# A two-block transformer stack on one core: gates as row tiles, values in turn, column sums in streamed form, and beta in VectorE's product ahead of the triangular solve

## What is computed

```python
# first block, recurrence: gates from two block-diagonal products of 64 x 64 blocks
r = sigmoid(block_diag(w_rg_r) @ x + b_rg_r)
i = sigmoid(block_diag(w_rg_i) @ x + b_rg_i)
# second block, mixer 0: gated delta rule, 8 heads of 128, chunks of 128 tokens
beta = sigmoid(b_raw)
g = -exp(a_log) * softplus(a_raw + dt_bias)          # b_raw, a_raw: 16 columns of hn @ w_in
gc = cumsum(g)
decay = exp(where(tri_incl, gc[:, None] - gc[None, :], -inf))
a_low = where(tri_strict, (k * beta) @ k.T * decay, 0)
sol = triangular_solve(a_low + eye, [v * beta, k * beta * exp(gc)], unit_diagonal=True)
```

## Time and profile before

| | |
|---|---|
| median of 3 runs | 1115.27 us (1115.21 to 1115.76) |
| profiled execution, its own time | 1115.75 us |
| its span, first to last instruction | 1114.0 us |
| TensorE busy, granted clock | 1103.2 us (99%), 0.998 of full speed |
| VectorE, ScalarE, GpSimd busy | 778.9, 596.5, 218.5 us |
| HBM read | 185.29 MB |

### The profile page before, as it was taken

One profiled execution on the slowest core, in us unless ns is written; L12 is line 12 of the kernel. 1 busy time (PEld: TensorE's weight loads), 2 busy tenths in 40 slices (PEclk: granted clock), 3 DMA queues, 4 the chain that ended last, 5 costly groups with the idle time before them and its releaser, 6 DMA issues.

```text
span 1114.0 us, 19328 instructions
## 1 busy us (share of the span) xinstructions
PE 1103.2 (99%) x7596; PEld 1012.0 (91%) x7596; DVE 778.9 (70%) x969; ACT 596.5 (54%) x806; POOL 218.5 (20%) x222
## 2 busy tenths in 40 slices
PE   9999999999999999999999999999999999999997
PEld 8999998889888889999999888888899999888887
DVE  7746985886877754599985877764467667777444
ACT  6547557645555543665764556643354446665332
POOL 2995003302000000167854010000010002000001
PEclk9999999999999999999999999999999999999999
DMA  9764442755555555445500356555545444656541
GB/s 287 240 219 152 154 140 89 229 185 188 190 188 188 188 193 189 148 138 188 176 29 1 114 172 197 191 195 188 189 152 189 152 151 151 204 190 210 189 151 39
DMA packets 155057, 187.28 MB, mean 168 GB/s; under 512 B 6608, under 2 KB 143984, under 8 KB 154992
## 3 DMA queue, kind: packets, MB, share of 16 engines
q1 hardware_dynamic: 151152, 183.80, 50.8%
q10 hardware_dynamic: 3840, 2.57, 0.8%
HBM read 185.29 MB, written 1.07 MB: 167 GB/s over the span
## 4 chain that ended last, share of the span: by engine, by line
PE 91%; DVE 4%; ACT 2%; POOL 2%; issue 1%; DMA 0%; POOLq 0%; SPq 0%; DVEq 0%; ACTq 0%
PE PS L475 24%; PE PS L525 12%; PE PS L480 12%; PE PS L406 7%; PE PS L407 7%; PE PS L408 7%; PE PS L527 6%; PE PS L354 2%; DVE WL L402 2%; PE PS L486 1%; PE PS L487 1%; PE PS L485 1%; PE PS L2165 1%; PE PS L2152 1%; PE PS L818 1%; DVE QKV L1725 1%
## 5 line engine op out<-in xcount | busy, mean ns | idle before, releaser
L402 DVE TENSOR_TENSOR WL<-RAW,WH 128x2048 fp32r<-128x2048 f32 x169 | 393.9, 2332 | 188.0 <-ACT WH L393 187.3
L393 ACT ACTIVATE WH<-RAW 128x2048 fp32r<-128x2048 f32 x169 | 323.1, 1912 | 190.8 <-PE PS L527 121.1
L475 PE MATMUL PS<-XHL,WH 128*128 128x512 f32 x976 | 336.4, 395 | 0.2 <-DVE WL L402 0.2
L480 PE MATMUL PS<-XHL,WL 128*128 128x256 f32 x976 | 261.6, 277 | 0.0
L475 PEld LDWEIGHTS PS<-XHL,WH 128*128 128x128 f32 x976 | 179.1, 188 | 38.1 <-DVE WL L402 0.4
L525 PE MATMUL PS<-HHL,WH 128*128 (+1 forms) x592 | 205.4, 394 | 0.0
L406 PE MATMUL PS<-XHL,WH 128*128 128x256 f32 x656 | 189.1, 288 | 0.0
L480 PEld LDWEIGHTS PS<-XHL,WL 128*128 128x128 f32 x976 | 183.3, 188 | 5.0
L407 PE MATMUL PS<-XHL,WH 128*128 128x256 f32 x656 | 185.5, 283 | 0.0
L408 PE MATMUL PS<-XHL,WL 128*128 128x256 f32 x656 | 185.5, 283 | 0.0
L527 PE MATMUL PS<-HHL,WL 128*128 (+1 forms) x592 | 164.0, 277 | 0.0
(11 more groups left out here) (345 smaller groups left out, 1695.1 us busy)
## 6 DMA issues: line engine op xcount, KB each, us to landing
RAW<-in_mlp_w_up SPq DMA_DIRECT2D x32, 1024.0 KB, 5.4
RAW<-in_mlp_w_down SPq DMA_DIRECT2D x32, 1024.0 KB, 4.9
RAW<-in_w_in SPq DMA_DIRECT2D x24, 1024.0 KB, 5.3
RAW<-in_w_ffn_in_pairs SPq DMA_DIRECT2D x22, 1024.0 KB, 5.1
RAW<-in_dn_w_in SPq DMA_DIRECT2D x16, 1024.0 KB, 5.8
RAW<-in_mb_w_in SPq DMA_DIRECT2D x12, 1024.0 KB, 5.2
RAW<-in_w_ffn_out SPq DMA_DIRECT2D x11, 1024.0 KB, 4.9
RAW<-in_w_in SPq DMA_DIRECT2D x16, 256.0 KB, 6.3
```

What stands on the lines that cost most here:

```text
L393: act.activation(WH[:, k], RAW[:, k], ACT.Copy).then_inc(hi_done, 1)
L402: dve.tensor_tensor(WL[:, k], RAW[:, k], WH[:, k].bitcast(F32), ALU.subtract).then_inc(lo_done, 1)
L475: pe.matmul(out, h[:, k, part], both[:, k].rearrange("p e t -> p (e t)"), start=(k == 0), stop=False, skip_group_check=True)
L480: mm = pe.matmul(out[:, TOK:512], l[:, low, part], both[:, low, 0], start=False, stop=(low == KB - 1), skip_group_check=True)
```

## The change

1. `WRI` holds, for each half of a block's rows, the two 64 x 64 blocks side by side, with their order swapped in the lower half. Two matmuls of 64 rows replace the two of 128; each writes a bank of its own (`gate_bank`). ScalarE reads four sigmoids of 64 x 256 a step. GpSimd no longer zeroes `WRI`, and SP doesn't wait for that.
2. In the value products of pairs 0 to 7 the heads alternate term by term.
3. The third norm's sums and beta's and decay's columns become one group of 16 matmuls, 32 output columns each (`WBS`) in four column tiles, over the squares and `H`, behind chunk 0. ScalarE copies the bank to `CS`; four small matmuls with a selection matrix (`SEL`) add the four tiles and turn them, in chunk 1 ahead of its tenth matmul. The rows (L662) come behind chunk 1 instead of in its middle. GpSimd prepares `SEL` and `WBS`.
4. The cumulative sum goes behind chunk 3, its copy behind VectorE's read-out of that step, its exponential to step 4 and `BEG` to step 5. TensorE's and VectorE's loops over dq are written out.
5. GpSimd's four products with `BRK2` go; VectorE multiplies key products, `BRK2` and `AM` in one instruction per system, 16 in all.
6. VectorE's read-out of the last dz bank goes behind two of the four odd-column steps, the small product ahead of them. TensorE waits for each bank where it uses it. ScalarE writes the even columns behind the third pair of exponentials, and three of the four silus stand inside the solve.

```diff
-    WRI = sb("WRI", [P, 2, KB, P], F32, Z + 72.25)
+    WRI = sb("WRI", [P, KB, P], F32, Z + 72.25)
+    WBS = sb("WBS", [P, KB, 32], F32, Z + 95)
+    CS = sb("CS", [P, 2, TOK], F32, Z + 84)
...
-        ROWS_AT = [4, 3, 2, 3, 4, 3]
+        ROWS_AT = [4, 3, 3, 3, 4, 3]
...
             elif m == 2:
+                pe.wait_ge(s_.prep, 1)
                 pe.wait_ge(s_.sq_done, 4 * m + 4)
-                for c in range(TT):
-                    for j in range(KB):
-                        mm = pe.matmul(PS[:, 4, 2 * c:2 * c + P].rearrange("p (r e) -> p r e", e=2), XN[:, j, c * P:(c + 1) * P],
-                                       W2[:, j, None, :].to_broadcast([P, P // 2, 2]), start=(j == 0), stop=(j == KB - 1))
+                for r, x in enumerate((XN, H)):
+                    for i in range(2):
+                        for g in range(4):
+                            mm = pe.matmul(PS[32 * g:32 * g + 32, 4, r * TOK:(r + 1) * TOK], WBS[:, 4 * i + g], x[:, 4 * i + g],
+                                           start=(i == 0), stop=(i == 1))
+                mm.then_inc(s_.col_sums, 1)
+                return
...
+        def column_sums(pe):
+            pe.wait_ge(s_.col_out, 1)
+            for c in range(TT):
+                mm = pe.matmul(PS[:, 4, 2 * c:2 * c + 2], CS[:, 0, c * P:(c + 1) * P], SEL[:, 16:18], start=True, stop=True)
+            mm.then_inc(s_.sum_done, 1)
+            for c in range(TT):
+                mm = pe.matmul(PS[:, 3, 256 + 16 * c:272 + 16 * c], CS[:, 1, c * P:(c + 1) * P], SEL[:, 0:16], start=True, stop=True)
+            mm.then_inc(s_.ba_done, 1)
...
         def norm_root(act, m):
+            if m == 2:
+                act.wait_ge(s_.col_sums, 1)
+                act.activation(CS[:].rearrange("p r t -> p (r t)"), PS[:, 4, :], ACT.Copy).then_inc(s_.col_out, 1)
...
+            order = [(e, b) for b in range(3) for e in range(2)] if n < 8 else [(e, b) for e in range(2) for b in range(3)]
+            for e, b in order:
+                mm = term(e, b, slice(P, TOK) if b else slice(0, P), b < 2, b != 1)
...
-            pool.wait_ge(s_.brk, 1)
-            for g in range(4):
-                am = AM[:, 4 * g:4 * g + 4]
-                pool.wait_ge(s_.d_done, 2 * g + 1)
-                pool.tensor_tensor(am, am, BRK2[:, 4 * g:4 * g + 4, None].to_broadcast([P, 4, P]), ALU.mult).then_inc(s_.ab_done, 1)
...
-                sigmoid(RR[:, j], PS[:, 3 + j % 2, 0:TOK], vec("b_rg_r", j)).then_inc(s_.gates_done, 1)
-                sigmoid(RI[:, j], PS[:, 3 + j % 2, TOK:512], vec("b_rg_i", j)).then_inc(s_.gates_done, 1)
+                for r, (out, bias) in enumerate(((RR, "b_rg_r"), (RI, "b_rg_i"))):
+                    for e in range(2):
+                        at = 64 * (r ^ e)
+                        rows_ = slice(64 * e, 64 * e + 64)
+                        sigmoid(out[rows_, j], PS[at:at + 64, gate_bank(j, e), 0:TOK], vec(bias, j)[rows_]).then_inc(s_.gates_done, 1)
...
                 if st.i is None and st.j == 1:
                     act.wait_ge(s_.ba_done, 1)
+                    act.wait_ge(s_.rc_ready, 3)
...
+                        if g == 0:
+                            even_columns()
...
+            gate_silu(0)
...
+                if 2 <= n < 5:
+                    gate_silu(n - 1)
...
                 dve.wait_ge(s_.gk_done, g + 1)
-                dve.wait_ge(s_.ab_done, g + 1)
-                dve.tensor_tensor(AM[:, r], AM[:, r], four(UB[g]), ALU.mult).then_inc(s_.a_done, 1)
-            steps(dve, seg["dq"], dq, head=3, tail=3)
+                dve.wait_ge(s_.d_done, 2 * g + 1)
+                for e in range(4):
+                    n = 4 * g + e
+                    ins = dve.scalar_tensor_tensor(out=AM[:, n], in0=four(UB[g])[:, e], scalar=BRK2[:, n:n + 1], in1=AM[:, n],
+                                                   op0=ALU.mult, op1=ALU.mult)
+                ins.then_inc(s_.a_done, 1)
+            steps(dve, seg["dq"], dq, head=6, tail=3)
...
+            dve.wait_ge(s_.l2sd, 1)
+            ch(dve.tensor_tensor(BRK[:], BETA[:], RK[:], ALU.mult))
             ch.wait(dve)
             dve.wait_ge(s_.ty_even, 1)
             for g in range(4):
+                if g == 2:
+                    gate_rows(Step(seg["dz"], 3, None))
                 dve.wait_ge(s_.ct_done, g + 1)
...
-                    pe.wait_ge(s_.gates_done, 2 * j - 2)
-                for r in range(2):
-                    mm = pe.matmul(PS[:, 3 + j % 2, r * TOK:(r + 1) * TOK], WRI[:, r, j], XN[:, j], start=True, stop=True)
+                    pe.wait_ge(s_.gates_done, 4 * j - 4)
+                for e in range(2):
+                    rows_ = slice(64 * e, 64 * e + 64)
+                    mm = pe.matmul(PS[:, gate_bank(j, e), 0:TOK], WRI[rows_, j], XN[rows_, j], start=True, stop=True)
```

More of the change, by code:

```diff
@@ L834, in attn_pv, with term @@
                 pe.wait_ge(s_.ol_done, 9 if n == 11 else n)
[L835 to L840, removed]
+            pt = turned_to(n)
+            two_heads = list(heads(n))
+            def term(e, b, out, start, stop):
+                _, _, _, vc, to = two_heads[e]
+                return pe.matmul(to[:, out], VT[:, b // 2, vc], queries(pt[:, e, P * b:P * b + P], n), start=start, stop=stop,
+                                 skip_group_check=True)
+            order = [(e, b) for b in range(3) for e in range(2)] if n < 8 else [(e, b) for e in range(2) for b in range(3)]
+            for e, b in order:
+                mm = term(e, b, slice(P, TOK) if b else slice(0, P), b < 2, b != 1)
             mm.then_inc(s_.pv_done, 1)
@@ L1341, in dq @@
                     act.activation(AROW[:], AROW[:], ACT.Exp).then_inc(s_.sm_ready, 1)
-                if st.i is None and st.j == 2:
+                if st.i is None and st.j == 4:
                     act.wait_ge(s_.gc_done, 1)
@@ L1378, in _, with gate_silu @@
                             act.activation(d[:, 4 * g:4 * g + 4], d[:, 4 * g:4 * g + 4], ACT.Exp).then_inc(s_.d_done, 1)
[L1380 to L1382 removed]
+                        if g == 0:
+                            even_columns()
             act.wait_ge(s_.brk, 1)
             act.activation(RK[:], RK2[:], ACT.Sqrt).then_inc(s_.l2sd, 1)
[L1386 removed]
+            def gate_silu(j):
                 zs = ZS[:, 2 * j:2 * j + 2]
@@ L1815, in _ @@
                         key_products(g)
[L1816 to L1817 removed]
+                    break
+                gate_rows(st)
                 if st.j < 2:
@@ L2005, in body @@
                     multiply(pe, st, XH, XL, None if st.j else (s_.xl_ready, 4 * m), tokens_out,
-                             between=lambda: norm_point(pe, m, 2 * st.j))
+                             between=lambda: norm_point(pe, m, 2 * st.j),
+                             beside=(lambda: column_sums(pe)) if m == 2 and st.j == 1 else None)
                     norm_point(pe, m, 2 * st.j + 1)
@@ L2085, in dq @@
                 times_x(2)(st)
-                if st.i is None and st.j == 1:
-                    for c in range(TT):
-                        for k in range(KB):
-                            mm = pe.matmul(PS[:, 3, 256 + 16 * c:384 + 16 * c].rearrange("p (r e) -> p r e", e=16),
-                                           H[:, k, c * P:(c + 1) * P], WBA[:, k, None, :].to_broadcast([P, KB, 16]),
-                                           start=(k == 0), stop=(k == KB - 1))
-                    mm.then_inc(s_.ba_done, 1)
-                if st.i is None and st.j == 2:
+                if st.j == 3:
                     pe.wait_ge(s_.g_ready, 1)
                     pe.matmul(PS[:, 3, 320:336], TRI[:], GT[:], start=True, stop=True).then_inc(s_.gc_sum, 1)
-            steps(pe, seg["dq"], dq, head=3, tail=3)
+            steps(pe, seg["dq"], dq, head=6, tail=3)
             for st in (Step(seg["dz"], j, None) for j in range(4)):
@@ L2129, in _, with banks_free @@
                 mm.then_inc(s_.ct_done, 1)
-            for k in range(SLOTS):
+            def banks_free(k):
                 pe.wait_ge(freed[k], uses_upto(seg["dz"], k))
             def level_x(n):
+                if n == 0:
+                    banks_free(2)
                 pe.wait_ge(s_.yf_out, n + 1)
```

78 lines of the change are left out of this document (41 added, 37 removed).

## The result

The changed kernel takes 1109.31 us (median of 5 runs, 1109.25 to 1109.55), the kernel before on the same chip 1115.41 us: a ratio of 0.9945 (95% interval 0.9935 to 0.9956), 6.1 us less. Its profiled execution took 1109.55 us with a span of 1107.8 us, 6.2 us under the span of before, at a granted clock of 0.999.

A forecast was written before the change was run, and what follows sets the result against it. TensorE, at 91% of the span, was taken to bound the kernel. Savings of 1.1 (gates), 2.1 (values), 1.45 (sums) and 1.75 us (z to the solve) sum to 6.4 us: 1115.27 to 1108.9 us, range 1105.6 to 1112.6.

The forecast's parts named there:

- Gates in row tiles: qk loop: two half-array matmuls take 0.72 us instead of 0.86, eight steps save 1.1 us (0.2 to 3.4).
- Values in turn: Value products of eight head pairs: alternating heads removes a 0.28 us offset, saving 2.1 us (0.8 to 3.4).
- Streamed sums: Third mixer's sums, beta and decay columns: TensorE gives back 3.9 us, of which 1.45 us comes through (0.3 to 3.9).
- Rival 2: Third mixer: TensorE gets the whole of the sums, 3.9 us instead of 1.45, giving 1106.4 us; chance 0.12.
- z to the solve: Last z chunk to second packed product: idle time behind GpSimd's beta products goes, saving 1.75 us (0.7 to 1.9).
- Rival 4: Before the solve: VectorE's 16 products take 1.45 us each, making the kernel slower at 1126.4 us; chance 0.03.
- Rival 1: Third mixer's chunks: VectorE keeps all the time freed by the sums, total gain 4.95 us, 1110.3 us; chance 0.16.
- Rival 3: Gates and values: mode switch leaves row tiles 0.2 us, values stay as they are; 1111.1 us, chance 0.16.

The follow-up runs named there:

- The pairs: Changed kernel with the gate matmuls of two steps together behind every second chunk, one array switch for both: 1110.87 us, ratio 0.9958 to the kernel before.
- squares first: Changed kernel with ScalarE's square of the keys ahead of the tap that waits for VectorE's last read-out: 1108.95 us, ratio 0.9940 to the kernel before.

## Why the prediction was right

The time came out 0.4 us above the forecast of 1108.9 us, well inside the range. The mechanisms are in the main the ones that it named, but part of the closeness is luck: the gates gave 0.8 us less than forecast, and 0.15 us more from the sums, 0.2 us more from the stretch into the solve and 0.27 us at the start, which the change does not explain, made up for most of it. By its steps:

**Gates in row tiles: right in sign, a quarter of the size.** 0.3 us instead of 1.1. The failed step is the choice of 0.72 us from the interval 0.72 to 0.84. The trace has 0.63 us from the gates to the next chunk, 0.09 us more ahead of them and 0.1 us behind: 0.82 us against 0.86. The argument for the low end, that the tiled sums of 256 columns carry an overhead of 0.3 us, was taken from a switch to column tiles; the scores, the only row-tiled block of before, pointed to the other end, and the overhead did not shrink with the columns. The pairs measure it apart: a second pair of gates behind the same switch adds 0.43 us, so the block is 0.43 us of columns and 0.4 us of switch. Here the rule of the Trainium skill quoted with the prediction (TensorEngine Tiling (Array Packing), Key Properties) agrees with the trace, and the sum by it, 0.2 us, was nearer to the measured 0.3 us than mine.

**Values in turn: right.** 0.27 us a step (1.08 to 0.81), eight times, and putting back the order alone gives it back.

**Streamed sums: the total right, its parts not.** 1.6 us for 1.45. The tiled block took 455.81 - 453.94 + 0.09 and 0.1, 2.06 us for 2.05. The small matmuls took 0.9 us instead of 1.2 (457.80 - 456.99, and 0.08): priced from one that stood alone. Each is two records in the profile, and in a row these start every 0.09 us at 2 columns and every 0.11 us at 16, where 0.13 us was assumed. VectorE's split for the fifth chunk ended at 476.04 us, which in the time of the kernel before (the sums start 2.63 us later there) is 478.7 us, as worked out; but TensorE was there at 474.78, in that time 477.4 and not 478.0, so the stall was 1.3 us and not 0.8. The product of 0.81 us that was to come back at step 5 took 0.15 us. And the sums behind the first z chunk came at 531.40 where 531.1 was worked out. The step itself, that VectorE is next in line and keeps over half of the sums, is shown twice: 4 us more work on TensorE cost 1.3 us, and an earlier start for VectorE gave 2.9 us. Rival 2 needed that earlier start.

**z to the solve: right in size, too simple in cause.** 2.86 us for 3.0. Two rows of VectorE's timeline, twelve of the 16 products and the small product:

```profile
551.86 3.18 DVE L1844 SCALAR_TENSOR_TENSOR AM<-PS,BRK,AM 128x128 f32<-128x128 f32 x12
554.96 0.16 DVE L1876 TENSOR_TENSOR BRK<-BETA,RK 128x16 f32<-128x16 f32 x1
```

The products take 3.18 / 12 = 0.26 us each, not 0.2: the prediction divided 1.15 us by columns, while the shortest instruction of the line that it took them from lasts 0.265 us. They end at 555.0 us, just as TensorE's last z chunk does (554.97), not 0.55 us ahead of it: the cover that the prediction named is used up, as "squares first" showed when TensorE came 1.5 us sooner and waited. Rival 4 (a blocked product of 1.45 us) did not come about, though GpSimd's copies run beside them. The prediction put the old idle time down to GpSimd and let the rest follow; undone one at a time, beta gives back 0.87 us and the silus 1.25 us.

**Rivals.** Rival 1 is out: VectorE did not keep everything. Rival 3 was right in one half, the row tiles at 0.3 us, and wrong in the other: the values did shrink. Its 1111.1 us needed both.

**The 0.27 us at the start** is not explained by the change: the same code moved by more between two profiles.

## What to carry to other kernels

When work leaves the engine that bounds, look first at what the next engine waits for before its own list begins: here one constant, the place of four transposes, was worth 2.9 us, where the work saved ahead of it brought 1.6. A switch of the array's tiling has a price that does not shrink with the block, so put more blocks behind one switch, but not where the last of them heads another engine's chain. And undo the parts of a reordering together as well as singly, since their prices need not add up: here 0.87 and 1.25 us made 2.38 us, and what was left of the reordering was slower than the old order.

## What the runs showed of the hardware

- A block of gates in row tiles cost about 0.4 us beyond its columns, at both sizes that ran: 0.82 us with 0.43 us of columns, 1.25 us with 0.86 us.
- In the kernel before, the second head's first product starts 0.28 us behind the first head's while later products of the first head still come after it; products that alternate between two column tiles take 0.81 us, the same in sequence per tile 1.07 us.
- Small VectorE products are seen at very different lengths: the same 16-column product took 1.45 us beside GpSimd's copies, 0.16 us where no copy ran, and 0.28 us in the middle of such copies with beta back on GpSimd (556.97), so the copies alone don't set its length. The 8-column one took 0.81 us, ending as GpSimd's instruction did (481.21 and 481.18 us), and 0.15 us with GpSimd idle. The products with one input from PSUM kept 0.26 us beside the same copies.
- The first 20 us of the same code vary by over 0.3 us between profiles (18.37 and 18.74 us), which is as much as the smallest term here.
